# RWKV inverse in 32-column blocks: Q by 64x64 tiles with 32 columns streamed, V by 32x32 tiles, GpSimd masks the scores and copies W's diagonal blocks

## The reference

```python
def step(S, inp):
    r_t, w_t, k_t, v_t, kk_t, a_t = inp
    sa = -jnp.einsum('dbhvk,dbhk->dbhv', S, kk_t)
    S = (S * w_t[..., None, :] + sa[..., :, None] * (kk_t * a_t)[..., None, :]
         + v_t[..., :, None] * k_t[..., None, :])
    return S, jnp.einsum('dbhvk,dbhk->dbhv', S, r_t)
```

## Time and profile before

| | us |
|---|---|
| median of 3 runs | 2788.41 (2785.87 to 2789.18) |
| profiled execution | 2788.39 |
| its span, first to last instruction | 2786.3 |
| TensorE busy (matmuls) | 2625.2 |
| VectorE busy | 1942.2 |
| ScalarE busy | 1185.9 |
| GpSimd busy | 272.1 |
| RWKV sweep | 357 to about 690 |

### The profile page before, as it was taken

The page is one execution under the profiler, slowest core; times in us unless marked ns, Lnnn a source line. Parts: engine busy times, 40 slices in busy tenths (PEclk is TensorE's granted clock), DMA queues, the critical chain, the costliest instruction groups (busy, mean ns, idle before and its releaser), DMA issues. The chain is left out here.

```text
span 2786.3 us, 40763 instructions
## 1 busy us (share of the span) xinstructions
PE 2625.2 (94%) x17014; PEld 2151.8 (77%) x17014; DVE 1942.2 (70%) x1885; ACT 1185.9 (43%) x1375; POOL 272.1 (10%) x199
## 2 busy tenths in 40 slices
PE   3999979998999999999999899999999999999996
PEld 3888857776777888888888678888778888888885
DVE  5788856666566888888888878865668755555557
ACT  2555544445444333333333345555443333333332
POOL 0000000000004000000000085641040000000000
PEclk9999989999999999999999999999999999999998
DMA  8899743230647888888888366744468755555552
GB/s 308 313 331 344 287 136 129 97 120 16 241 164 262 327 304 328 303 323 307 317 312 308 121 227 242 271 155 160 166 231 323 253 193 191 186 195 186 190 193 79
DMA packets 259411, 636.60 MB, mean 228 GB/s; under 512 B 10607, under 2 KB 17445, under 8 KB 239173
## 3 DMA queue, kind: packets, MB, share of 16 engines
q1 hardware_dynamic: 253106, 621.84, 62.7%
q10 hardware_dynamic: 6162, 12.72, 1.2%
HBM read 632.42 MB, written 2.10 MB: 228 GB/s over the span
## 5 line engine op out<-in xcount | busy, mean ns | idle before, releaser
L521 DVE TENSOR_TENSOR s_wl<-s_raw,s_wh 128x2048 fp32r<-128x2048 f32 (+1 forms) x393 | 914.5, 2327 | 513.6 <-ACT s_wh L516 504.8
L516 ACT ACTIVATE s_wh<-s_raw 128x2048 fp32r<-128x2048 f32 x396 | 758.5, 1916 | 1080.8 <-PE pa L726 412.7
L724 PE MATMUL pa<-s_wh,s_hth 128*128 128x512 f32 x1312 | 526.2, 401 | 14.8 <-DVE s_wl L521 7.9
L725 PE MATMUL pa<-s_wl,s_hth 128*128 128x512 f32 x1312 | 515.1, 393 | 0.0
L726 PE MATMUL pa<-s_wh,s_htl 128*128 128x512 f32 x1312 | 514.8, 392 | 0.0
L724 PEld LDWEIGHTS pa<-s_wh,s_hth 128*128 128x128 f32 x1312 | 248.9, 190 | 76.7 <-DVE s_wl L521 13.1
L726 PEld LDWEIGHTS pa<-s_wh,s_htl 128*128 128x128 f32 x1312 | 248.7, 190 | 53.7
L725 PEld LDWEIGHTS pa<-s_wl,s_hth 128*128 128x128 f32 x1312 | 249.4, 190 | 48.7
L724 PE MATMUL pb<-s_wh,s_hth 128*128 128x512 f32 x704 | 274.1, 389 | 0.0
L726 PE MATMUL pb<-s_wh,s_htl 128*128 128x512 f32 x704 | 273.9, 389 | 0.0
L725 PE MATMUL pb<-s_wl,s_hth 128*128 128x512 f32 x704 | 273.9, 389 | 0.0
(11 more groups left out here) (398 smaller groups left out, 3482.4 us busy)
## 6 DMA issues: line engine op xcount, KB each, us to landing
s_raw<-in_ffn_w_in SPq DMA_DIRECT2D x176, 1024.0 KB, 5.2
s_adaw<-in_ada_w SPq DMA_DIRECT2D x144, 1024.0 KB, 6.0
s_raw<-in_ffn_w_out SPq DMA_DIRECT2D x88, 1024.0 KB, 7.7
s_raw<-in_ab_w_in SPq DMA_DIRECT2D x48, 1024.0 KB, 9.8
s_raw<-in_diff_w_in SPq DMA_DIRECT2D x48, 1024.0 KB, 5.2
s_adaw<-in_ada_w SPq DMA_DIRECT2D x48, 512.0 KB, 6.1
s_raw<-in_ab_w_out SPq DMA_DIRECT2D x16, 1024.0 KB, 5.3
s_qkv<-in_ada_w SPq DMA_DIRECT2D x16, 1024.0 KB, 7.2
```

Source lines behind the costliest of these rows:

```text
L516: act.activation(wh[:, s % 2, :, 0:width], raw[:, s, :, 0:width], ACT.Copy).then_inc(hi_done, 1)
L521: dve.tensor_tensor(wl[:, s % 2, :, 0:width], raw[:, s, :, 0:width], wh[:, s % 2, :, 0:width].bitcast(F32), ALU.subtract).then_inc(lo_done, 1)
L724: pe.matmul(o, a_hi, w_hi, start=start and k == 0, stop=False)
L725: pe.matmul(o, a_hi, w_lo, start=False, stop=False)
```

## The change

`LEVELS` is 5. V, W and Q keep only the 32 columns of a row's own 32-block: `R_W`, `R_V` and `R_Q` are [128, 8, 32] instead of [128, 8, 64].

- GpSimd (`diagonal`) multiplies `R_GA`'s first half, 128x512, with a mask of the diagonal 32-blocks into the new `R_D`. It waits for VectorE's second mask of the scores and for the last Q piece of the pair before.
- VectorE's `first` adds the two column halves of C0 and then an identity (two additions of 128x256 instead of one of 128x512), and makes V itself by a transpose. TensorE's `first` is left for pair 0 alone; for the others ScalarE's `seed` writes V into bank `L2`, where it had copied V out.
- Levels 1 to 4: `level_q` multiplies `R_D` with V, 16 calls with 64 columns of weights and 32 streamed. `level_v` is 32 calls on 32x32 tiles, the four blocks of each unit on the array's diagonal. Masks, copies and transposes have 256 columns instead of 512.
- The last level joins the 32-blocks: `cross_q` and `cross_w`, 16 calls each on 32x32 tiles off the diagonal, into quarter columns. VectorE only negates `cross_q`'s result. ScalarE's `last_seed` is gone. Its `last_w` copies four blocks of 32x128 into the off-diagonal blocks of `R_WF`, and GpSimd's `own_w` copies W's own blocks, four copies of 32x256, into the diagonal ones. `R_WF` is zeroed once.
- The reciprocal roots of GpSimd are queued behind `own_w` of the pair after and `diagonal` of the next but one. The GLA's `gla_turn` takes the banks in another order. The table of constants has 320 columns less.

```diff
+            def own_w(t):
+                pool.wait_ge(diag_ready, t + 1)
+                pool.wait_ge(wt_ready, 4 * t + 4)
+                if t:
+                    pool.wait_ge(u_done, 4 * t)
+                for h in range(2):
+                    for b in range(2):
+                        r = quad(h, b)
+                        ins = pool.tensor_copy(R_WF[r, :, b * HB:(b + 1) * HB], R_W[r])
+                ins.then_inc(own_ready, 1)
+
+            def diagonal(n):
+                pool.wait_ge(g_ready, 4 * n + 2)
+                if n:
+                    pool.wait_ge(own_ready, n)
+                    pool.wait_ge(q_done, 5 * n - 1)
+                pool.tensor_tensor(R_D[:], R_GA[:, n % 3, :, 0:CH], own_block.unsqueeze(1).to_broadcast((P, NU, CH)),
+                                   ALU.mult).then_inc(diag_ready, 1)
...
+            for t in range(-1, PAIRS + 1):
+                if 0 <= t < PAIRS:
+                    own_w(t)
+                if t + 1 < PAIRS:
+                    diagonal(t + 1)
+                if t > 0:
+                    roots(t - 1)
...
-            def last_seed(t):
-
-                act.wait_ge(wt_ready, 4 * t + 4)
-                act.wait_ge(vc_ready, 5 * t + 5)
-                act.activation(L2, flat(R_W), ACT.Copy).then_inc(ws_ready, 1)
+            def seed(n):
+
+                act.wait_ge(first_ready, n + 1)
+                act.wait_ge(vc_ready, 4 * n)
+                act.activation(L2V, flat(R_V), ACT.Copy).then_inc(v_seeded, 1)
...
                 if n:
                     dve.wait_ge(w_done, n)
-                dve.tensor_tensor(R_W[:], R_C0[:], eye2.unsqueeze(1).to_broadcast((P, NU, CH)), ALU.add).then_inc(first_ready, 1)
+                    dve.wait_ge(own_ready, n)
+                dve.tensor_tensor(R_W[:], R_C0[:, :, 0:HB], R_C0[:, :, HB:CH], ALU.add)
+                dve.drain()
+                dve.tensor_tensor(R_W[:], R_W[:], eye4.unsqueeze(1).to_broadcast((P, NU, HB)), ALU.add)
+                dve.drain()
+                dve.transpose(flat(R_V), flat(R_W)).then_inc(first_ready, 1)
...
             def level_q(t, lv):
 
-                pe.wait_ge(vc_ready, 5 * t + lv)
+                if lv == 1:
+                    pe.wait_ge(first_ready, t + 1)
+                    pe.wait_ge(diag_ready, t + 1)
+                    pe.wait_ge(wf_ready, t)
+                else:
+                    pe.wait_ge(vc_ready, 4 * t + lv - 1)
                 for u in range(NU):
-                    mm = two(unit(L1, u), R_GA[:, t % 3, u, 0:CH], R_V[:, u], start=(u == 0))
+                    mm = two(quarter(L1Q, u), R_D[:, u], R_V[:, u], start=(u == 0))
                 mm.then_inc(q_done, 1)
...
                 for u in range(NU):
-                    mm = two(unit(L2, u), R_W[:, u], R_Q[:, u])
+                    for g in range(4):
+                        r = slice(g * HB, (g + 1) * HB)
+                        mm = pe.matmul(quarter(L2V, u)[r], R_W[r, u], R_Q[r, u], start=False, stop=True, skip_group_check=True)
                 mm.then_inc(v_done, 1)
...
+            def across(k):
+                for d in range(2):
+                    for h in range(2):
+                        yield d * NCH + k, h, quad(h, 1 - d), quad(h, d), 1 - d
+
+            def cross_q(t):
+
+                pe.wait_ge(vc_ready, 4 * t + 4)
+                pe.wait_ge(bonus_out, t + 1)
+                if t:
+                    pe.wait_ge(s_ready, 3 * t)
+                for k in range(NCH):
+                    for u, h, r, c, b in across(k):
+                        mm = pe.matmul(quarter(C2Q, k)[r], R_GA[c, t % 3, u, b * HB:(b + 1) * HB], R_V[c, u], start=(k == 0), stop=True,
+                                       skip_group_check=True)
+                mm.then_inc(q_done, 1)
+
+            def cross_w(t):
...
+                        mm = pe.matmul(quarter(L1X, k)[c], R_Q[r, k], R_W[r, u], start=(k == 0), stop=True, skip_group_check=True)
                 mm.then_inc(w_done, 1)
...
                 if i == 0:
                     pe.wait_ge(wf_ready, c + 1)
+                    pe.wait_ge(own_ready, c + 1)
```

More of the change, by code:

```diff
@@ L45 @@
 NU = 2 * NCH
-LEVELS = 6
+LEVELS = 5
+HB = 32
 DH = 16
@@ L258, in build_trunk, with quad, quarter @@
         heads1 = cst[:, C_HEADS:C_HEADS + P]
-        level_masks = cst[:, C_LEVEL:C_LEVEL + 2 * LEVELS * CH].rearrange("p (d l n) -> p d l n", d=2, l=LEVELS)
+        pair_mask = cst[:, C_LEVEL:C_LEVEL + 2 * CH].rearrange("p (d n) -> p d n", d=2)
+        level_masks = cst[:, C_LEVEL + 2 * CH:C_LEVEL + 2 * CH + 8 * HB].rearrange("p (d l n) -> p d l n", d=2, l=4)
         eye2 = cst[:, C_I2:C_I2 + CH]
[L263 to L267, removed]
+        eye4 = cst[:, C_FOLD:C_FOLD + HB]
+        own_block = cst[:, C_OWN:C_OWN + CH]
+        L1Q, L1X, L2V, C2Q = L1[:, 0:NU * HB], L1[:, W - NCH * HB:W], L2[:, 0:NU * HB], C2[:, 2 * CH:2 * CH + NCH * HB]
+        def quad(h, b):
+            return slice((2 * h + b) * HB, (2 * h + b + 1) * HB)
+        def quarter(bank, u):
+            return bank[:, u * HB:(u + 1) * HB]
         def both(row):
@@ L384, in build_trunk @@
         wt_ready = sem("wt_ready")
-        ws_ready = sem("ws_ready")
+        v_seeded = sem("v_seeded")
+        own_ready = sem("own_ready")
+        diag_ready = sem("diag_ready")
         wf_ready = sem("wf_ready")
@@ L1359, in _, with roots @@
             pool.memset(small[:, 95:96], -0.5)
+            pool.memset(R_WF[:], 0.0)
             pool.drain().then_inc(bd_zero, 1)
             half_neg = small[:, 95:96]
-            for c in range(PAIRS):
+            def own_w(t):
[15 more added lines that the diff above has]
+                                   ALU.mult).then_inc(diag_ready, 1)
+            def roots(c):
+                pool.wait_ge(own_ready, min(c + 2, PAIRS))
                 pool.wait_ge(ys_var, c + 1)
@@ L1736, in _ @@
                     z_copy(m)
-                if front:
-                    level_v(n, 0)
+                if front and n:
+                    seed(n)
                 if m < PAIRS:
@@ L2590, in level_v @@
                 pe.wait_ge(qc_ready, 5 * t + lv)
-                if lv > 1:
+                if lv == 1:
+                    pe.wait_ge(v_seeded, t + 1)
+                else:
                     pe.wait_ge(wt_ready, 4 * t + lv - 1)
                 for u in range(NU):
-                    mm = two(unit(L2, u), R_W[:, u], R_Q[:, u])
+                    for g in range(4):
+                        r = slice(g * HB, (g + 1) * HB)
+                        mm = pe.matmul(quarter(L2V, u)[r], R_W[r, u], R_Q[r, u], start=False, stop=True, skip_group_check=True)
                 mm.then_inc(v_done, 1)
-            def last_w(t):
+            def across(k):
+                for d in range(2):
+                    for h in range(2):
+                        yield d * NCH + k, h, quad(h, 1 - d), quad(h, d), 1 - d
[10 more added lines that the diff above has]
+            def cross_w(t):
                 pe.wait_ge(qc_ready, 5 * t + 5)
-                pe.wait_ge(ws_ready, t + 1)
-                for u in range(NU):
-                    mm = two(unit(L2, u), R_Q[:, u], R_W[:, u])
+                pe.wait_ge(wt_ready, 4 * t + 4)
+                for k in range(NCH):
+                    for u, h, r, c, b in across(k):
+                        mm = pe.matmul(quarter(L1X, k)[c], R_Q[r, k], R_W[r, u], start=(k == 0), stop=True, skip_group_check=True)
                 mm.then_inc(w_done, 1)
@@ L2896, in _ @@
                     rows_at(t, 3)
-                if front:
+                if n == 0:
                     first(n)
```

58 lines of the change are left out of this document (34 added, 24 removed).

## The result

The changed kernel takes 2772.99 us (median of 4 runs, 2770.53 to 2776.32) where the kernel before takes 2788.54 (2785.87 to 2789.18) beside it: a ratio of 0.9946, 95% interval 0.9934 to 0.9958. It is faster by 15.5 us. The forecast was 31 us, 2757.5; the sign and the range (2744 to 2775) hold, but the gain is half of what the sum said, and that the time lies in the range is luck: its upper end, 2764 to 2775, stood for tiles that run two side by side or dear changes of form, (b), and for late operations of VectorE and GpSimd, and most of what was lost went to neither. The profiled execution has a span of 2772.8 us.

The account below looks back on a forecast made before the run. TensorE, busy for 94% of the span, was taken to bound the kernel. Its terms summed to -4.0 us for a middle step (six times -24.0), with step 0, step 7 and the start -30.8 us: 2757.5 us, range 2744 to 2775.

Parts of the forecast that it names:

- (b): Rival: 32x32 tiles run only two side by side, or form changes cost double; 2773 us; 16%.
- Step 1: TensorE, each RWKV step: `first`, piece and wait together, goes from TensorE; -1.8 us.
- Step 2: TensorE's four V pieces on 32x32 tiles, four side by side: 0.51 us each instead of 0.93; -1.7 us a step.
- (d): Rival: the four tiles of a group run one after the other, 0.128 us; kernel slower, about 2810 us; 5%.
- Step 3: TensorE's fifth Q and last W piece, 16 calls each on 32x32 tiles: 0.26 instead of 0.93 us; -1.3 a step.
- Step 4: TensorE's four other Q pieces: half the columns streamed, weight loads still 64 columns; no gain taken, other bound -1.7 us.
- (a): Rival: weight loads don't bind, so the Q pieces halve too; 13 us less, 2745 us; 7%.
- Step 5: TensorE's changes of tile form, eight further ones a step at 0.12 or 0.14 us: +1.0, bounds 0.5 to 1.6.
- Step 6: TensorE's waits for ScalarE's copies of U and V get shorter: -1.0 us a step.
- Step 7 of the sum: TensorE gets a new wait before the next pair's scores, for VectorE's products: +0.8 us a step.
- Rival (c): Records can't be issued so fast over a whole piece; kernel some 2800 us, a little below that mean 2790; 6%.
- rival (e): Granted clock falls to 1.2 GHz in a stretch of the steps, some 3.5 us for each 7 us stretch; 3%.

Follow-up runs that it names:

- a4_first: a_cols4 with the seed of V for each pair made by TensorE again instead of ScalarE's copy: 2769.54 us, ratio 0.9929.
- a_small: Changed kernel with 28 of the 32 row loads cut to 64 of 2048 columns (rows computed from the rest are wrong): 2759.92 us, ratio 0.9905.
- b_fill: Kernel before with 96 already met waits on TensorE ahead of the third V piece of each pair: 2838.87 us, one time.
- b_fill_small: b_fill with the row loads cut to 64 columns (rows computed from the rest are wrong): 2840.05 us, one time.
- a4_again: a_cols4 timed once more, on the same chip as a4_later, as its reference: 2762.62 us, ratio 0.9917.
- a_cols4: Changed kernel, complete, each row load split by columns into four parts, the later ones each behind a later TensorE piece: 2761.65 us, ratio 0.9904.
- a4_later: a_cols4 with GpSimd's product (R_D) held back until VectorE's first operations for the pair are through: 2768.06 us, ratio 0.992.
- b_small: Kernel before with the same 28 row loads cut to 64 columns as in a_small: 2787.49 us, ratio 0.9998.
- b_cols4: Kernel before, complete, with its row loads in four gated parts as in a_cols4: 2788.86 us, ratio 0.9999.
- a_nogate: a_cols4 with the four parts of each load issued at once, without the waits between them: 2773.46 us, ratio 0.9943.
- a_half: Changed kernel, each row load split into two halves of 64 partitions, the second behind the Q piece one further on: 2784.71 us, ratio 0.9999.
- a_cols: Changed kernel, each row load split in two by columns, the second half behind the Q piece one further on: 2769.95 us, ratio 0.9942.

## Why the prediction was half right

**Step 1, -1.8 for `first`: right for the kernel before** (the piece is gone and nothing takes its place in the steps from 2 on). In tiles of the new form it would have been 0.7 (a4_first).

**Step 2, -1.7 for V: -1.5.** 0.56 us of pure advance instead of 0.51, 0.035 for a group instead of 0.032. Four 32x32 tiles do run side by side; rivals (b) and (d) fall.

**Step 3, -1.3: about right.** The last W piece is 0.26 us (0.38 with the change of form), the fifth Q 0.26 to 0.44.

**Step 4, nothing for Q: right.** 0.91 us from one Q piece to the next one of the same form, with half of the columns streamed. So the stream doesn't pace it, and (a) falls; that the weight loads do is the explanation left.

**Step 5, +1.0: about +0.8, an estimate.** 0.12 us behind a 32x32 piece (0.68 - 0.56), where the next pair of the same form comes after 0.05.

**Step 6, waits: right.** U's waits fell from 11.9 us in 18 to 7.3 in 18, 0.8 for a step. V's 7.7 us in 13 (before the first and the fifth Q piece) are gone, of which the sum has the first part in step 1.

**Step 7 of the sum, +0.8 before the scores: right.** 0.52 us in the rows above; in the steps of a_small 0.5 to 0.7, 1.0 in the one before the last.

The walk of a step was thus good to 0.15 us (32.55 against 32.4 in a_small). Three things failed, and the first one, which the sum doesn't have, took half of the gain.

**What was left out: the supply of instructions.** This is the step that failed: the prediction took the V pieces' 64 records for 32 as a cost of TensorE's time alone, named the DMA engines only as 0.38 busy, and put nothing in the sum for what TensorE's instructions need of them. Yet they come over these engines, one packet for some 256 records, and behind the loads. The waits for "issue" are 9.3 us from 372 to 665 us. There are also two stretches of 3.4 us at 1.2 GHz, where the kernel before is at 1.00 (for the second the prediction said 1.00, too: from 408 to 620 us; windows of the changed kernel; 0.57 is 3.4 of 4 us at half):

```profile
402.00:406.00 4.00, 3.62 (x39) 3.36 (x43) 1.55 (x4) 0.00 (x0) 1.57 (x4) 0.57 0.30 123
433.00:437.00 4.00, 3.99 (x96) 2.19 (x88) 3.58 (x7) 1.03 (x3) 0.00 (x0) 0.57 0.37 78
```

They cost at most 1.7 us each. Together that is 9.3 to 12.7 us, and a_small is 13.1 us faster than the changed kernel. The second one begins 3 us after the start of the stall of 2.0 us at 430 us, and that the clock falls behind idle time of TensorE is what b_fill and b_fill_small show; but behind the stalls of 1.8 and 1.2 us at 466 and 532 us it stayed at 1.00. The first one can't be put down to stalls: a4_again, with one wait of 0.4 us there, has the same at 404 us. Rival (c) named an issue limit, but as a pace over whole pieces, which isn't what happens: pieces run at full pace until the store is empty.

**"VectorE ... Cost nothing": wrong at the start.** Its product takes 1.80 us beside GpSimd's, 1.1 more than the sum had, and in the first two pairs nothing covers it. Waits of the changed kernel from 372 to 665 us:

```profile
PE pt L2633 <- DVE s_R_V L2072: 1.9, 1, 1.9
...
PE py L2523 <- DVE s_R_V L2072: 0.8, 1, 0.8
```

Step 0 gave between nothing and 1.0 us instead of 3.3 (27.41 us between bonus pieces in a_small and 26.22 in a_cols4, 27.09 and 27.19 in the kernels before with the same loads), step 1 2.6 instead of 4.0 (33.21 against 35.85). The waits of 1.9 and 0.8 us are a part of that, and with the two products apart V's are 1.2 and 0.8 us shorter (a4_later). The clock is another part of step 0; windows of it in a_small and b_small:

```profile
378.47:405.88 27.41, 23.76 (x703) 18.50 (x701) 18.04 (x35) 12.76 (x26) 2.83 (x5) 0.94 0.06 17
```

```profile
379.61:406.70 27.09, 25.21 (x542) 20.43 (x540) 19.31 (x34) 14.86 (x28) 0.00 (x0) 0.99 0.06 16
```

At 0.94 of the clock a_small loses up to 1.6 us there, b_small up to 0.3. From step 2 on VectorE's delay is hidden, as the prediction said. The prediction asked whether GpSimd's product ends in time, and not what it does to VectorE. The Trainium skill says it, in "SBUF — State Buffer", section "Who interferes with whom": an operation of VectorE with two inputs in SBUF contends with one of GpSimd that reads SBUF, and the shared ports are an exclusive lock, so the second one waits for the first. The trace agrees: 1.80 is a little less than 1.27 + 0.69.

**The last pair's step gave a little more, not less.** From the first to the last bonus piece, steps 0 to 6, the profiled execution of a_small takes 222.2 us and that of b_small 243.7, 21.5 less where 27.3 were forecast; ahead of them it gains 1.1. From the last bonus piece to the last product with the state, step 7, it gains 3.7 (62.1 to 58.4), and a_cols4 5.6 against b_cols4 (61.2 to 55.7), where 3 were forecast. The clock blurs this: rival (e) was real there, with 20 us at 1.2 GHz in a4_later and 6.8 us in the changed kernel (from 617 us) and in a_small (from 607 us), and none before 641 us in a_cols4.

The sum with what was measured: 30.8 us forecast, 27.6 without the loads, 15.5 with them.

## What to carry to other kernels

Where a change puts more and shorter matmuls into the same time, count instructions as bytes that must come over the DMA engines: look for instruction packets that start right behind large loads, for waits inside pieces that end a fixed time after such a packet's start, and at how many instructions ran since the last one. Near the limit, give large loads out in small parts between the pieces of TensorE; here that brought back 11 of the 15 us by which the change fell short (2773 to 2762 us), and nothing where the limit wasn't near (b_cols4). And before an operation goes to an idle GpSimd, see what VectorE does at the same time with two inputs.

## What the runs showed of the hardware that was not expected

- An instruction packet (16 KB, 0.9 us or more) starts behind the load that was issued to the DMA engines before it: in the changed kernel 22 of 40 packets between 400 and 600 us start within 0.31 us of the last 8 KB row of a load, with at most six of its 128 rows behind them, and none starts in a load's middle. Issuing the load as four transfers at once changed nothing.
- A TensorE that has run dry goes on 2.2 to 3.0 us after the start of an instruction packet: all 39 waits for "issue" of 0.2 us and more from 372 to 665 us in the changed kernel, a_nogate, a_half and a_cols end so. It ran dry 399 to 497 matmuls and weight loads after the start of the packet before (five stalls of the changed kernel); in other runs some stalls began after fewer, down to 366.
- Behind each idle stretch of 4.6 us of TensorE the granted clock fell from 2.4 to 1.2 GHz for 3.4 to 6.8 us (b_fill, b_fill_small, seven times each).
- A load to 64 partitions takes as long as one of twice the bytes to 128 (5.5 and 5.0 us from issue to landing).
- Four 32x32 tiles of fp32 with 32 columns: 0.035 us for a group of four, 9 ns for a record, over a whole piece.
- A wait that is already met takes TensorE 48 ns (4.6 us for 96, b_fill).
- VectorE's product of two inputs in SBUF took 1.80 us beside one of GpSimd that took 1.27, and 0.69 apart from it.
